# Two convolution-and-attention layers: depthwise taps divided anew between the engines, and another order of projections, staging and scaling

## The reference

```python
h = _rmsnorm(x, g_mix[l]);  p = h @ w_in[l]
c_q = _rmsnorm(p[..., :o1], g_q[l]);  q = (c_q @ w_uq[l]).reshape(b, s, 8, 64 + 32)
q_nope, q_rope = q[..., :64], _apply_rope(q[..., 64:], cos_h, sin_h)
c_kv = _rmsnorm(p[..., o1:o2], g_kv[l]);  kv = (c_kv @ w_ukv[l]).reshape(b, s, 8, 64 + 64)
k_nope, v = kv[..., :64], kv[..., 64:]
k_rope = _apply_rope(p[..., o2:o3], cos, sin)
y_attn = _mla_attention(q_nope, q_rope, k_nope, k_rope, v)   # softmax over all 512 keys
a, gt = jnp.split(p[..., o3:], 2, axis=-1);  u = a * jax.nn.sigmoid(gt)
u = _dwconv(u, w_dw_conv[l], b_dw_conv[l])                   # depthwise, 31 taps, 512 channels
u = jax.nn.silu(_layernorm(u, g_conv_ln[l], b_conv_ln[l]))
x = x + jnp.concatenate([y_attn, u], axis=-1) @ w_o[l]
```

## Time and profile before

| | us |
|---|---|
| median of 3 runs | 2169.49 |
| lowest and highest | 2167.78, 2169.55 |
| the profiled execution, its own time | 2169.24 |
| its span | 2167.5 |

### The profile page before, as it was taken

The page is one execution under the profiler, slowest core; times in us unless marked ns, Lnnn a source line. Parts: engine busy times, 40 slices in busy tenths (PEclk is TensorE's granted clock), DMA queues, the critical chain, the costliest instruction groups (busy, mean ns, idle before and its releaser), DMA issues.

```text
span 2167.5 us, 26197 instructions
## 1 busy us (share of the span) xinstructions
PE 1959.6 (90%) x8323; PEld 1560.3 (72%) x8323; DVE 1276.9 (59%) x1958; ACT 1011.0 (47%) x1807; POOL 283.6 (13%) x216
## 2 busy tenths in 40 slices
PE   7999989889999989768799999999957699999997
PEld 6777768668878867545578888787735477888786
DVE  4453356453333355899657666536699857666634
ACT  4554464344443334567554343434557644343432
POOL 0001000010000001356310000001246501000000
PEclk8999989999999999878999999999989999999999
DMA  3121112223322222211022333223210023333222
GB/s 127 46 68 63 59 41 79 78 74 96 97 92 95 96 66 74 49 25 35 25 89 87 102 92 103 92 97 85 64 27 25 20 74 88 102 92 102 93 97 83
DMA packets 148117, 162.30 MB, mean 75 GB/s; under 512 B 34104, under 2 KB 102670, under 8 KB 148044
## 3 DMA queue, kind: packets, MB, share of 16 engines
q1 hardware_dynamic: 148044, 161.38, 24.9%
HBM read 159.24 MB, written 2.10 MB: 74 GB/s over the span
## 4 chain that ended last, share of the span: by engine, by line
PE 75%; DVE 19%; ACT 4%; issue 1%; DMA 0%; ACTq 0%; POOL 0%; SPq 0%; DVEq 0%
PE bank_a L1840 13%; PE bank_a L1842 12%; PE bank_a L1841 12%; PE bank_b L1840 11%; PE bank_b L1842 11%; PE bank_b L1841 11%; DVE arena L1207 6%; DVE w_lo L1204 2%; DVE h_lo L1204 2%; DVE arena L1699 2%; DVE arena L1204 2%; DVE soft L1691 1%; PE bank_a L1927 1%; DVE x_t L1204 1%; DVE h_lo L1207 1%
## 5 line engine op out<-in xcount | busy, mean ns | idle before, releaser
L1204 DVE TENSOR_TENSOR w_lo<-w_raw,w_hi 128x512 fp32r<-128x512 f32 (+3 forms) x617 | 446.5, 733 | 707.4 <-ACT w_hi L931 383.1
L931 ACT ACTIVATE w_hi<-w_raw 128x512 fp32r<-128x512 f32 (+3 forms) x392 | 232.4, 604 | 449.5 <-PE bank_b L1842 228.9
L1840 PE MATMUL bank_b<-h_hi,w_hi 128*128 128x512 f32 x816 | 321.8, 394 | 4.4 <-DVE var L1222 3.9
L1840 PE MATMUL bank_a<-h_hi,w_hi 128*128 128x512 f32 x720 | 285.2, 396 | 40.4 <-DVE h_lo L1207 20.4
L1841 PE MATMUL bank_b<-h_lo,w_hi 128*128 128x512 f32 x816 | 318.8, 391 | 0.0
L1842 PE MATMUL bank_b<-h_hi,w_lo 128*128 128x512 f32 x816 | 318.7, 391 | 0.0
L709 ACT ACTIVATE w_hi<-w_raw 128x512 fp32r<-128x512 f32 x225 | 140.4, 630 | 326.9 <-PE bank_a L1842 180.4
L1841 PE MATMUL bank_a<-h_lo,w_hi 128*128 128x512 f32 x720 | 283.8, 394 | 0.0
L1842 PE MATMUL bank_a<-h_hi,w_lo 128*128 128x512 f32 x720 | 283.4, 394 | 0.0
L1207 DVE SCALAR_TENSOR_TENSOR arena<-arena,cols_all 128x512 f32<-128x512 f32 x272 | 233.9, 912 | 0.0
L1840 PE MATMUL bank_a<-split,w_hi 128*128 128x512 f32 x420 | 170.0, 405 | 33.8 <-DVE split L1204 25.6
(11 more groups left out here) (234 smaller groups left out, 2725.3 us busy)
## 6 DMA issues: line engine op xcount, KB each, us to landing
w_raw<-in_w_up_dram SPq DMA_DIRECT2D x240, 256.0 KB, 3.1
w_raw<-in_w_down_dram SPq DMA_DIRECT2D x152, 256.0 KB, 2.8
w_raw<-in_w_in_dram SPq DMA_DIRECT2D x64, 256.0 KB, 2.9
w_raw<-in_w_gate_dram SPq DMA_DIRECT2D x32, 256.0 KB, 2.6
w_raw<-in_w_o_dram SPq DMA_DIRECT2D x32, 256.0 KB, 2.8
w_raw<-in_w_out_dram SPq DMA_DIRECT2D x16, 256.0 KB, 2.9
w_raw<-in_w_in_dram SPq DMA_DIRECT2D x16, 192.0 KB, 2.4
w_raw<-in_w_in_dram SPq DMA_DIRECT2D x16, 144.0 KB, 2.1
```

The source lines that it names most:

```text
L931: nc.scalar.activation(w_hi[:, s, 0:c], w_raw[:, s, 0:c], ACT.Copy).then_inc(w_round, 1)
L1204: return nc.vector.tensor_tensor(out_, a, b, op)
L1840: nc.tensor.matmul(out_, a_hi, b_hi, start=start, stop=False, skip_group_check=loose)
```

## The change

1. The taps: 23 on DVE, 8 on PE, none on ACT and POOL. POOL multiplies the identity with a tap's 128 coefficients (diagonals) and PE multiplies this diagonal matrix, in plain float32, with the shifted input (conv_taps), adding 8 taps in PSUM. ACT copies the sum out with the bias (base), DVE's odd taps add to it, and DVE joins the accumulators. Tile 0's 8 matmuls stand among the key projection's chunks, tile 1's around the first two scores, those of tiles 2 and 3 in steps 0 to 13 of the loop.
2. Keys first: the order is M_A, M_G, M_KV, M_Q, then a new M_V, then pair by pair one chunk of keys and three of queries. The key projection goes to bank_a, the query projection to bank_b. The squares of the key latent are taken from PSUM without the input's norm, which is put into the variance instead (epsv).
3. The queries' norm is not applied to the latent; it is multiplied into the rotation table once (trig_q), and this table multiplies each pair's queries. The second head's columns are ordered with the rotated part first, so a second table and copies of the shared key on the other half of the partitions are made (copy_key).
4. All heads' values are projected at once before the loop, tokens on the partitions (M_V), with no transposition, into a buffer whose other halves are zero; the two heads of a pair add up in one PSUM bank, which is rounded straight from there (round_out). values2 issues one matmul a step, six steps late (PV_LAG).
5. The keys of a pair are one projection (6 matmuls instead of 12).
6. ACT instead of DVE scales the probabilities. On DVE the taps now stand last in a step. PE's transposition is that of block g - 1 and stands last.
7. The mean over channels stands behind the first output chunk.

The core of the diff:

```diff
-POOL_TAPS = 17
-DVE_TAPS = CONV_K - POOL_TAPS
+PE_TAPS = 8
+DVE_TAPS = CONV_K - PE_TAPS
+PV_LAG = 6
+CONV_STEPS = ({}, {}, {g: 1 for g in range(8)}, {8: 1, 9: 1, 10: 1, 11: 1, 12: 2, 13: 2})
...
+                def diagonals(j):
+                    for r in range(PE_TAPS):
+                        if j > 0:
+                            pool.wait_ge(diag_used, was[diag_used.name] + (j - 1) * PE_TAPS + r + 1)
+                        c = L_TAP + j * 32 + DVE_TAPS + r
+                        nc.gpsimd.tensor_scalar(diag[:, r, :], ident[:, :], cols_all[:, l, c:c + 1], None,
+                                                ALU.mult).then_inc(diag_made, 1)
...
 # ACT, step g
+                    if 1 <= g <= BLOCKS:
+                        b = (g - 1) % TT
+                        act.wait_ge(p_step, was[p_step.name] + g)
+                        nc.scalar.activation(prob[:, b, :], prob[:, b, :], ACT.Copy,
+                                             scale=soft[:, 3, b:b + 1]).then_inc(p_ready, 1)
...
+                    if i + 1 < PAIRS:
+                        if m == 1:
+                            stage_k(i + 1)
+                        if m in (4, 5):
+                            stage_q(i + 1, m - 4)
+                        if 1 <= m <= 3:
+                            split2(M_PAIR + (i + 1) * SLOTS + m)
+                        if m == 4:
+                            split2(M_PAIR + (i + 2) * SLOTS)
...
 # DVE, step g
-                        dve.wait_ge(p_step, was[p_step.name] + g)
-                        nc.vector.tensor_scalar(prob[:, b, :], prob[:, b, :], soft[:, 3, b:b + 1], None,
-                                                ALU.mult).then_inc(p_ready, 1)
-                    taps(taps_by(g) - tap)
                     if i + 1 < PAIRS:
+                        if m == 1:
+                            stage_k_lo(i + 1)
                         if m == 4:
-                            make_q(i + 1, next_banks[0])
...
+                            make_q(i + 1, 0)
+                            make_q(i + 1, 1)
+                            split2_lo(M_PAIR + (i + 2) * SLOTS)
+                        if m == 5:
+                            stage_q_lo(i + 1, 0)
+                            stage_q_lo(i + 1, 1)
+                        if 1 <= m <= 3:
+                            split2_lo(M_PAIR + (i + 1) * SLOTS + m)
...
+                    if g < BLOCKS:
+                        taps(taps_by(g, first_taps) - tap)
...
 # PE
+                def conv_taps(j, taps):
+                    for r in taps:
...
+                        pe.wait_ge(diag_made, was[diag_made.name] + j * PE_TAPS + r + 1)
+                        nc.tensor.matmul(conv_banks[j], diag[:, r, :], upad[:, j, DVE_TAPS + r:DVE_TAPS + r + S],
+                                         start=r == 0, stop=r == PE_TAPS - 1).then_inc(diag_used, 1)
```

More of the change, by code:

```diff
@@ new lines, in _ @@
+                nc.scalar.activation(conv_odd[1], conv_banks[0], ACT.Copy).then_inc(conv_base, 1)
+                for k in range(1, 4):
+                    split2(M_Q + k)
+                for t in range(KVT):
+                    square(bank_a[:, t, :], t, sq0 + KT, added0 + KT - 1)
+                split2(M_Q + 4)
+                act.wait_ge(kr_step, was[kr_step.name] + 4)
+                nc.scalar.activation(kr_hi[ND:P, :], rot[ND:P, 0, :], ACT.Copy).then_inc(kr_round, 1)
+                split2(M_Q + 5)
@@ new lines, in _, with copy_key @@
+                rsqrt_guess(norm0 + 2)
+                split2(M_Q + 6)
+                split2(M_Q + 7)
+                for t in range(KVT):
+                    act.wait_ge(cn_ready, was[cn_ready.name] + t + 1)
+                    nc.scalar.activation(lat_hi[:, QT + t, :], ckv_f[:, t, :], ACT.Copy).then_inc(lat_round, 1)
+                for k in range(KVT):
+                    split2(M_V + k)
+                split2(M_PAIR)
+                def copy_key(q, hd):
+                    if q == 0 and hd == 0:
+                        act.wait_ge(kr_ready, was[kr_ready.name] + 1)
+                        act.wait_ge(w_used, was[w_used.name] + M_Q + KT)
+                    rows = slice(ND, P) if hd == 0 else slice(0, ND)
+                    for part, full in ((kk_hi, kr_hi), (kk_lo, kr_lo)):
+                        nc.scalar.activation(part[q][hd][rows, :], full[ND:P, :].bitcast(F32), ACT.Copy).then_inc(kr_copied, 1)
@@ L1035, in stage_v @@
[L1035 to L1050 removed]
+                        rows = slice(hd * ND, hd * ND + ND)
@@ new lines, in _ @@
+                for k in range(6, KT):
+                    split2_lo(M_KV + k)
+                    taps(2)
+                split2_lo(M_Q)
+                taps(10)
+                for k in range(1, 4):
+                    split2_lo(M_Q + k)
+                    taps(1)
+                dve.wait_ge(w_used, was[w_used.name] + M_KV + KT)
+                stt(krf[ND:P, :], bank_a[ND:P, 2, :], 1.0 / MLA_SCALE, norm[ND:P, :], ALU.mult, ALU.mult).then_inc(proj_out, 1)
+                dve.wait_ge(proj_out, was[proj_out.name] + 8 + 1)
@@ L2140, in _ @@
-                for k in range(QT):
-                    queries(0, k, first_banks[0])
-                total(bank_b[:, 3, :], added0 + KT + QT + KVT - 3)
-                pe.wait_ge(var_ready, norm0 + 2)
-                for hd in range(2):
-                    keys(0, hd, first_banks[1][hd])
-                values_of(0, first_banks[2])
+                    last.then_inc(w_used, 1)
+                pe.wait_ge(conv_base, was[conv_base.name] + 1)
+                total(bank_b[:, 3, :], added0 + KT - 1 + KVT - 1 + QT - 1)
@@ L2148, in scores2 @@
+                pe.wait_ge(lat_ready, was[lat_ready.name] + KVT + QT)
+                keys(0)
+                for k in range(QT):
+                    queries(0, k)
                 def scores2(g):
```

611 lines of the change are left out of this document (313 added, 298 removed).

## The result

The changed kernel takes **2196.74 us** (median of 4 runs, 2195.23 to 2198.05), the kernel before 2168.81 in the same comparison (2167.78 to 2169.55): ratio 1.0129, 95% interval 1.0111 to 1.0146. It is slower by 28 us. Forecast were 2158.5, range 2126 to 2179. The profiled execution spans 2194.1 us, against 2167.5.

A forecast was written before the change was run, and what follows sets the result against it. DVE, stretched by POOL, was taken to bound the loop. Before the loops -16.4, loops -0.5, ends -1.8, diagonals +2, clock +6: together -10.7 from 2169.24, giving 2158.5 us, range 2126 to 2179.

The forecast's parts named there:

- POOL's additions stretched DVE: Block loop: a DVE tap takes 0.66 us alone, 1.7 inside POOL's burst, 1.285 on average.
- D: Rival: in the loop 1.285 us is a tap's own price, 43 us a layer more, 2244 us; chance 0.02.
- DVE's work in the loop: Block loop, one layer: 91 us of work for DVE, against 121 busy in the kernel before.
- PE's work at full clock: Block loop, one layer: PE's operations total 93 us, or 108 at the clock granted before (0.86).
- The piece before the loop: From the keys' projection start to the first row maximum: 59.7 us, a gain of 8.2 a layer.
- rival C: Before the loop: keys first buys nothing, the query norm's chain leaves gaps as long; 2175 us; chance 0.10.
- The loop's order: Block loop: splits and remainders before taps wait for ACT; steps sum to 127.3 us, against 125.95 and 129.14.
- the taps behind the remainders: DVE's staging steps in the loop: two taps add 1.32 us before the next maximum, at T+4.6.
- The end: After the last row maximum, until the last value matmul: 6.9 us against 7.80.
- The clock: PE's granted clock: a term of +6 us in the sum.
- Rival B: Block loop: PE on its low clock becomes the bound, from 0.75 downwards; slower, 2180 us; chance 0.14.
- +3 and +0.5 us: Loop, pairs 1 and 2: short steps outrun PE, so the copy before key staging is late by this much.

The follow-up runs named there:

- e11: The kernel before with POOL's additions cut to 16 of 512 columns, every wait and other operation kept: 2107.67 us.
- e6: The changed kernel with 24 additions of 128x512 added on POOL in each loop, behind its diagonals: 2204.14 us.
- e4: The changed kernel with splits one step ahead, transposition right behind the scores, and taps ahead of splits and remainders: 2125.40 us.
- e2: The changed kernel with PE's transposition of block g - 1 moved right behind the scores: 2170.17 us.
- e3: The changed kernel with DVE's taps moved right behind the reciprocal, ahead of splits and remainders: 2159.06 us.
- e5: The changed kernel with the loop's 16 diagonal matmuls a layer covering only 16 of 512 columns: 2186.28 us.
- e7: The kernel of e4 with the probabilities scaled on DVE again instead of ACT: 2124.49 us.

## Why the prediction was wrong

**What was right.** POOL's additions stretched DVE: shown from both sides by e11 and e6. A tap alone takes 0.66 us, and D fell. DVE's work in the loop: 91 forecast, 86.3 measured. PE's work at full clock: 93 forecast, 90.5 in e4's second loop (clock 1.00). The last pair, where PE has no projections: 24 us forecast, 24.1 measured (first to last maximum of the pair).

**Right in size, cause open.** The piece before the loop took 61.91 us against 59.7 forecast, a gain of 6.0 a layer instead of 8.2, and rival C's time (no gain) is out. But the forecast gave this gain to the order, keys first, and e11 has the old order with 59.45 us once POOL's additions are short. No run has the new order beside POOL's additions, so how much of the 6.0 us belongs to the order is not shown.

**The step that failed** is "The loop's order", the ladder (the sum of steps, maximum to maximum) of 127.3 us; measured were 145.6 and 140.6. By pairs, layer 0: 42.0, 43.6, 35.9 and 24.1, where the ladder had 32.4, 36.7, 34.2 and 24. It let ACT's copy follow the scaling at once, and gave PE's lateness 3.0 and 0.5 us, in the short steps alone. But in every step the transposition stands last on PE, behind scores, queries, values and diagonals, and PE's queries themselves wait for a split that ACT makes behind that copy. I had not seen that the splits stood a pair ahead of their use in the kernel before, and that the change moved them into the step that uses them. e2, where the transposition is on time, has loops of 132.6 and 131.7 us: the ladder is then off by 5, most of it in pair 0 (36.8 for 32.4), where I left out ACT's copies of the shared key (L1023, 1.2 us in each of two steps) and the wait of DVE's first taps in step 0 for ACT's base of tile 1 (2.2 us); these two are read from the rows and were not tested by a run.

**Inside the ladder** stood the cost that proved largest, the taps behind the remainders, at 1.32 us a staging step, some 24 us a layer over 18 such steps. It was priced and let stand, because the ladder came out as long as the loop before; e3 shows it at 37.7 us in both layers together.

**The end**: 6.9 forecast, 10.83 measured in layer 0. DVE's last reciprocal stood behind two taps and a join, and ACT's last scaling waited for it; and 5 value matmuls, not 4, stand behind the last transposition. The timeline, DVE and then ACT:

```profile
1072.49 1.41 DVE L1241 SCALAR_TENSOR_TENSOR arena<-arena,cols_all 128x512 f32<-128x512 f32 x2
1073.93 0.69 DVE L1238 TENSOR_TENSOR arena<-arena 128x512 f32<-128x512 f32 x1
1074.54 0.15 DVE L1753 RECIPROCAL soft<-soft 128x1 f32<-128x1 f32 x1
```

```profile
1074.73 0.72 ACT L1098 ACTIVATE arena<-arena,soft 128x512 f32<-128x512 f32 x1 [1.11 <-DVE soft L1753]
```

**The small terms.** The clock stands in the sum with +6 us, and no run shows that term by itself. What the runs show is a clock of 0.86 and 0.92 in the loops as they ran, lowest in the first pair (0.76), and 0.97 and 1.00 once the waits were gone (e4). Most diagonals took POOL 0.60 us, where 0.4 was taken; what the 16 of them cost on the path is not shown either.

**Rival B** came nearer with its 2180 us than the forecast, but by luck. Its condition (0.75 or less over the loop) was not met, and its reason, the amount of PE's work, is refuted by e2 and e5.

**The chances**: slower had 0.22, nearly all of it on B and C. A rival "the copy waits for PE's last piece" was half in the text, as +3 and +0.5 us, and should have been carried through all steps.

## What to carry to other kernels

When three engines hand work round within one software-pipelined step, write for each engine's queue what stands last in it and who waits for that; an engine at 75% busy can hold the loop with one late piece. Put the piece that others wait for first (here scores, then transposition), put filler (taps, values, diagonals) where the engine would wait, and let nothing be made in the step that uses it. Then an exchange such as matmul taps for POOL's additions pays: the same parts in another order gave 2125 us instead of 2197, and with 6 taps on PE 2115, 2.5% under the kernel before. The order is to be settled before the exchange is judged: e11's 2107.67 us shows what was there to win, and the changed kernel's 2196.74 says nothing against the exchange.

## What the runs showed of the hardware

POOL's 128x512 additions stretch DVE's operations by the place of their operands. In e6, beside them, a tap (two tensors in SBUF) went from 745 ns to 1525, a TENSOR_SCALAR from SBUF to SBUF from 487 (e7's scaling) to 1261, and an addition of two SBUF tensors from 690 (the join at 1073.93) to 1411 (the last two are single operations), while the row maximum (683 ns), a remainder read from PSUM (688) and products with a PSUM operand (675) kept their times. The sentence that the prediction weighed speaks of two-port modes only; the Trainium skill (SBUF — State Buffer, section "SBUF: two separate sides") also names a DVE operation with two SBUF inputs, against a GpSimd operation that reads SBUF, as one that takes the shared ports for its whole length. The trace agrees with this second wording in that the taps are stretched (745 to 1525 ns); that the ports are held for an operation's whole length is seen in no row.

PE's granted clock rose from 0.86 and 0.92 to 0.97 and 1.00 when its gaps were closed (e4), and did not rise when its work was cut with the gaps left (e5: 0.85 and 0.84). Less work for PE did not give it a better clock here; fewer waits did.
